# Rows brought back tile by tile at the head of the next layer, routing scratch moved, four experts with fixed weights

## What is computed

```python
y = grouped_expert_mlp(xt, expert_idx, weights, lp['e_wg'], lp['e_wu'], lp['e_wd'])
# per expert e, on the tokens sent to it: (silu(x @ wg[e]) * (x @ wu[e])) @ wd[e]
x = x + g1 * mix
x = x + g2 * hierarchical_moe(rms_norm(x, lp['norm2']) * (1 + sc2) + sh2, lp)
```

## Time and profile before

| | us |
|---|---|
| median of 3 runs (lowest, highest) | 1497.56 (1494.43, 1499.7) |
| profiled execution, its own time | 1498.07 |
| its span, first to last instruction | 1496.3 |
| PE busy | 1251.5 (84%) |
| DVE, ACT, POOL busy | 707.0, 282.6, 113.4 |
| moved by DMA | 334.61 MB, mean 224 GB/s |
| granted TensorE clock, mean | 0.92 |

### The profile page before, as it was taken

One profiled execution on the slowest core, in us unless ns is written; L12 is line 12 of the kernel. 1 busy time (PEld: TensorE's weight loads), 2 busy tenths in 40 slices (PEclk: granted clock), 3 DMA queues, 4 the chain that ended last, 5 costly groups with the idle time before them and its releaser, 6 DMA issues.

```text
span 1496.3 us, 20523 instructions
## 1 busy us (share of the span) xinstructions
PE 1251.5 (84%) x7762; PEld 860.0 (57%) x7762; DVE 707.0 (47%) x1553; ACT 282.6 (19%) x708; POOL 113.4 (8%) x171
## 2 busy tenths in 40 slices
PE   5999999889977799879739999988798569988781
PEld 2765677557863455556337556766587345655450
DVE  2256866782356133223252686677444613333224
ACT  0211233651111000000022104256221100000000
POOL 2000000000001111111100000000100011111100
PEclk7999999999977999999969999999999569999896
DMA  9221101356058999999651110023913199999975
GB/s 386 108 88 57 57 1 57 120 197 269 29 197 357 414 419 420 420 416 412 244 225 54 63 57 29 1 84 150 367 71 113 49 416 419 418 420 418 405 293 225
DMA packets 58179, 334.61 MB, mean 224 GB/s; under 512 B 11392, under 2 KB 11392, under 8 KB 23900
## 3 DMA queue, kind: packets, MB, share of 16 engines
q1 hardware_dynamic: 42336, 294.94, 48.8%
q0 software_dynamic: 15744, 38.34, 6.6%
HBM read 322.41 MB, written 27.61 MB: 234 GB/s over the span
## 4 chain that ended last, share of the span: by engine, by line
PE 50%; DMA 21%; DVE 11%; SPq 7%; issue 4%; ACT 2%; DVEq 2%; PEld 1%; POOL 0%; ACTq 0%; PEldq 0%; POOLq 0%
PE bank L1616 12%; PE bank L1560 8%; DMA ring<-in_stream 8%; PE bank L1985 7%; PE bank L1875 7%; SPq L350 6%; DMA RAB<-in_stream 6%; PE bank L2019 5%; DMA mod_rows<-RAB 2%; DMA U<-in_stream 2%; DMA RAB<-mod_rows 2%; DMA U<-moe_out 1%; PE bank L1717 1%; PE bank L1891 1%; DVE U L1168 1%
## 5 line engine op out<-in xcount | busy, mean ns | idle before, releaser
L1985 PE MATMUL bank<-U,HT 128*64 128x256 f32 (+2 forms) x1088 | 205.4, 411 | 12.5 <-DMA RAB<-in_stream 4.7
L1985 PE MATMUL bank<-ring,HT 128*64 128x256 f32 (+2 forms) x736 | 143.3, 434 | 46.0 <-DMA RAB<-in_stream 27.7
L1616 PE MATMUL bank<-HT,ring 128*128 128x512 f32 (+1 forms) x640 | 175.4, 435 | 2.0 <-issue 2.0
L1985 PEld LDWEIGHTS bank<-U,HT 128*64 128x64 f32 (+2 forms) x1088 | 131.2, 154 | 51.0 <-issue 26.4
L1875 PE MATMUL bank<-ring,HT 128*128 128x256 f32 x640 | 148.7, 394 | 13.3 <-DVE U L1219 7.7
L1560 PE MATMUL bank<-ring,HT 128*128 128x256 f32 x640 | 149.1, 385 | 3.0 <-ACT HT L603 3.0
L1875 PEld LDWEIGHTS bank<-ring,HT 128*128 128x128 f32 x640 | 125.7, 199 | 33.0 <-issue 10.0
L1616 PEld LDWEIGHTS bank<-HT,ring 128*128 128x128 f32 x640 | 97.3, 191 | 79.7 <-issue 79.7
L1985 PEld LDWEIGHTS bank<-ring,HT 128*64 128x64 f32 (+2 forms) x736 | 85.6, 154 | 91.8 <-issue 70.9
L1560 PEld LDWEIGHTS bank<-ring,HT 128*128 128x128 f32 x640 | 119.4, 192 | 18.6 <-issue 3.7
L1008 DVE SCALAR_TENSOR_TENSOR U<-U,prm 128x655 f32<-128x655 f32 x120 | 107.8, 899 | 6.3 <-issue 0.4
(11 more groups left out here) (346 smaller groups left out, 1590.4 us busy)
## 6 DMA issues: line engine op xcount, KB each, us to landing
ring<-in_stream SPq DMA_DIRECT2D x162, 1024.0 KB, 18.7
U<-in_stream SPq DMA_DIRECT2D x90, 1024.0 KB, 28.0
RAB<-in_stream SPq DMA_DIRECT2D x14, 1024.0 KB
U<-moe_out SPq DMA_DIRECT2D x20, 512.0 KB, 7.6
RAB<-mod_rows POOLq DMA_DIRECT2D x12, 512.0 KB, 11.9
moe_in<-CAT POOLq DMA_DIRECT2D x10, 512.0 KB, 3.2
X<-in_x SPq DMA_DIRECT2D x1, 2560.0 KB, 15.0
out_y<-X SPq DMA_DIRECT2D x5, 512.0 KB, 6.9
```

The source lines that it names most:

```text
L1616: ins = e.matmul(out, wt(q)[:, k, P * (n % 2):P * (n % 2) + P], HT[:, k, lo:lo + w], start=(k == 0), stop=(k == KD - 1))
L1985: ins = e.matmul(PS[2 + p][s, FF * j:FF * j + FF], xgT[:, p, k, s], wt(key)[:, k, :], start=(k == 0), stop=(k == KD - 1))
```

## The change

1. `FIXED` is 4: experts 0 to 3 have F blocks, only four B blocks are left for the largest ranked experts, and the order is `FPPFPPBPFFPQBQBBPP` (F in rounds 0, 3, 8 and 9). Twelve tiles (0 to 11) come first in SP's order.
2. SP loads tiles 5 to 10 without `lanes_rdy`, tile 11 after `h2_rdy` of all five token tiles, tile 12 after `lanes_rdy`, tile 13 after `mod_st`. The waits for `ov_go` and `wslot_ps` ahead of tile 11 are gone; `ov_go` is waited for after the last expert tile.
3. The table's scratch (`over`, `masked`, `place16`, `blockno`, `rows16`, `place`, `wblk`, `cmp`) lies in `HT`, whose content is dead by then. `lanes` is made right after the ranks instead of after the slots. The float32 `place` is written by ACT as a copy of `place16` (new semaphore `place_rdy`) in place of DVE's compare.
4. The adds of the rows for layer 0 move to the head of layer 1 and run tile by tile between squares, roots, scaling, transposes and projection tiles.

```diff
-FIXED, BIGS, MIDS, SMALLS = 2, 8, 16, 8
+FIXED, BIGS, MIDS, SMALLS = 4, 8, 16, 8
-ROUNDS = list("QFPPFBPPPBPBBQBBPP")
+ROUNDS = list("FPPFPPBPFFPQBQBBPP")
...
-                for i in range(EXT, 3 * FIXED):
+                for i in range(EXT, RING + EXT):
+                    load_expert(i)
+                e.wait_ge(S["h2_rdy"], NT * (l + 1))
+                for i in range(RING + EXT, 3 * FIXED):
                     load_expert(i)
                 e.wait_ge(S["lanes_rdy"], l + 1)
-                for i in range(3 * FIXED, RING + EXT):
-                    load_expert(i)
-
-                e.wait_ge(S["ov_go"], l + 1)
-                e.wait_ge(S["wslot_ps"], l + 1)
-                for i in range(RING + EXT, PLACES - 1):
+                for i in range(3 * FIXED, PLACES - 1):
                     load_expert(i)
                 e.wait_ge(S["mod_st"], 64 * (l + 1))
...
+                if l:            # ACT
+                    squares(0)
+                    normed_out(0)
+                    for t in range(1, 4):
+                        squares(t)
+                    qkv_out(0)
+                    normed_out(1)
+                    normed_out(2)
+                    squares(4)
+                    qkv_out(1)
+                    qkv_out(2)
+                    normed_out(3)
+                    normed_out(4)
...
+                e.wait_ge(S["slot_rdy"], l + 1)
+                A(place, place16, ACT.Copy).then_inc(S["place_rdy"], 1)
...
+                if l:            # DVE; rows_back(0, l - 1) and modc stand ahead
+                    norm1(0, 1)
+                    scaled(0)
+                    rows_back(1, l - 1)
+                    evac1(0)
+                    rows_back(2, l - 1)
+                    rows_back(3, l - 1)
+                    norm1(1, 2)
+                    scaled(1)
+                    scaled(2)
+                    evac1(1)
+                    evac1(2)
+                    rows_back(4, l - 1)
+                    norm1(3, 2)
+                    scaled(3)
+                    scaled(4)
+                    evac1(3)
+                    evac1(4)
...
+                if l:            # PE
                     normed_tile(l, 0)
+                    qkv_tile(0)
                     normed_tile(l, 1)
+                    normed_tile(l, 2)
+                    qkv_tile(1)
+                    qkv_tile(2)
+                    normed_tile(l, 3)
+                    normed_tile(l, 4)
+                    qkv_tile(3)
```

More of the change, by code:

```diff
@@ L611, in qkv_out, with squares @@
                     A(qkv[:, t, :], PS[4 + t % 2][:], ACT.Copy).then_inc(S["pj_sb"], 1)
[L613 to L616, removed]
+                def squares(t):
+                    e.wait_ge(S["x_rdy"], NT * (l - 1) + t + 1)
+                    A(nrow2, X[:, t, :], ACT.Square, accum_out=small(1400 + t, 1))
+                    e.drain()
+                    e.drain().then_inc(S["sq_rdy"], 1)
+                if l:
[11 more added lines that the diff above has]
+                    normed_out(4)
+                else:
+                    normed_out(0)
+                    normed_out(1)
+                    for t in range(NT - 2):
                         qkv_out(t)
@@ L884, in _, with norm1 @@
             for l in range(DEPTH):
+                def norm1(t0, n):
+                    e.wait_ge(S["sq_rdy"], (3 + NT) * l - NT + t0 + n)
+                    rs(n, 1.0 / D, 1400 + t0)
                 if l:
-                    e.wait_ge(S["sq_rdy"], 4 * l)
-                    rs(NT, 1.0 / D)
-                    scaled(0)
-                    scaled(1)
+                    rows_back(0, l - 1)
                 e.wait_ge(S["ld_par"], 16 * (l + 1))
@@ L904, in evac1 @@
                     ins.then_inc(S["hT_d"], 1)
-                for t in range(NT):
-                    evac1(t)
-                    if t + 2 < NT:
-                        scaled(t + 2)
+                if l:
[16 more added lines that the diff above has]
+                    evac1(4)
+                else:
+                    for t in range(NT):
+                        evac1(t)
+                        if t + 2 < NT:
+                            scaled(t + 2)
                 e.wait_ge(S["dt_act"], 3 * l + 2)
@@ L1321, in _ @@
                 e.tensor_scalar(small(1660, NE), rank, float(BIGS), 2.0, ALU.min, ALU.mult); dr()
+                e.tensor_tensor_reduce(small(1280, NE), key, iota[:, 0:NE], 1.0, 0.0, ALU.mult, ALU.add, lane)
                 e.tensor_tensor(capm, capm, step, ALU.add)
                 e.tensor_tensor(at0, at0, small(1660, NE), ALU.add); dr()
-                e.tensor_scalar(at0, at0, float(QUART), None, ALU.mult)
+                e.tensor_scalar(lane, lane, 3.0, float(experts(l)), ALU.mult, ALU.add)
+                e.tensor_scalar(at0, at0, float(QUART), None, ALU.mult); dr()
+                e.tensor_copy(lanes[:], lane).then_inc(S["lanes_rdy"], 1)
                 nov, cs, cs2 = small(1280, NE), small(1320, 16 + NE), small(1370, 16 + NE)
@@ L1368, in _ @@
                                 ALU.mult).then_inc(S["slot_rdy"], 1)
-                lane = small(1279, 1)
-                e.tensor_scalar(key, rank, rowno[:, 0, 0:1], -1.0, ALU.subtract, ALU.is_equal); dr()
-                e.tensor_tensor_reduce(capm, key, iota[:, 0:NE], 1.0, 0.0, ALU.mult, ALU.add, lane); dr()
-                e.tensor_scalar(lane, lane, 3.0, float(experts(l)), ALU.mult, ALU.add); dr()
-                e.tensor_copy(lanes[:], lane).then_inc(S["lanes_rdy"], 1)
                 for j in range(before_slots(l) - 1):
```

65 lines of the change are left out of this document (34 added, 31 removed).

## The result

| | before | after |
|---|---|---|
| median of 20 runs, us | 1498.01 | 1489.26 |
| lowest, highest | 1494.36, 1506.89 | 1482.94, 1497.39 |
| recorded ratio to before, 95% interval | | 0.9936, 0.9920 to 0.9951 |
| profiled execution, its own time (span) | 1498.07 (1496.3) | 1485.86 (1484.1) |
| PE busy, granted clock | 1251.5, 0.92 | 1248.4, 0.93 |

A forecast was written before the change was run, and what follows sets the result against it. The prediction took the weight stream to bound each expert stage. Seam 3, layer 1's stream 8 and layer 0 -1.5 sum to 9.5 us off 1498.1, giving 1488.6, as a median 1488.0; range 8 in 10: 1481 to 1496.

The forecast's parts named there:

- The bound: Each layer's expert stage is bound by the weight stream; its end depends on when the stream becomes continuous and bytes left.
- Seam, start: Between the layers: the first projection tile of layer 1 starts about 11.5 us after the first add, 10.3 us earlier.
- Seam, the wait of 4 us ahead of tile 1: Between the layers: PE waits some 4 us ahead of the second projection tile, since DVE's program sets tile 1.
- Seam, size: Between the layers: tile-by-tile work brings L1589 4.6 us earlier, less a clock charge; gain 3, between 1.5 and 4.6.
- The charge of 1.5 us for the low clock: In the seam: one projection tile after a wait runs at the lower clock, taking 1.5 us off the 4.6 gained.
- Layer 1's stream, size: Layer 1's expert stage: the weight stream becomes continuous earlier; gain 8 us, between 3 and 11.
- Layer 1's stream, cause: Tiles 6 to 11 skip `lanes`: tile 13 saves 5.7 us, `mod_st` 5.1; about 3 given back by rounds starting with F.
- it doesn't do what it says: Rival, 7%: early fixed tiles buy nothing as they block places; layer 1 gains 0, layer 0 loses 2.5; 1497.
- Layer 0's expert stage: Layer 0's stream was already full, so only the order changes: 1.5 us lost, bounds 0 and 3.
- My own mark for a wrong forecast: Expert stages: wrong if DMA share falls below 0.95 in rounds 1 to 8, the write stays at 9, or overflow rounds appear.
- The slower rival: Rival, 5%: five rolling places starve the stream in rounds 1 and 2, 19 us a layer, 38 in all: 1526.
- The sum: Whole kernel: 3 + 8 - 1.5 = 9.5 us off 1498.1 gives 1488.6, median 1488.0; the forecast keeps 55%.

## Why the forecast held, step by step

- **The bound**: right. Both expert stages follow the weight stream; what moved them was when it became continuous.
- **Seam, start** (forecast: projection tile 0 about 11.5 us after the first add): right, 11.6.
- **Seam, the wait of 4 us ahead of tile 1**: wrong. Tile 0 ended 21.7 us after the first add and not 18.3, since it ran at 0.70; and tiles 1 and 2 were scaled at 20.5 and not 22.0, since the roots of tiles 1 and 2 start as soon as DVE is done with the adds; I had them wait for a square, but the square that they need, tile 2's, is done by then. The two errors meet: projection tile 1 starts at 24.2 us (forecast 24.6), tile 2 ends at 38.2 (forecast 38.2, both without the charge for the clock). That they meet is luck.
- **Seam, size** (forecast 3, of 1.5 to 4.6): L1641 at 47.8 us after the first add; over all traces with the new seam 46.2 to 47.8, mean 47.4, for 52.2 to 53.4 with the old, mean 52.9, so 5.5 us, above the bounds. The charge of 1.5 us for the low clock was about right: it costs 1.6 by the estimate above. The term that was mis-sized is DVE's way to tiles 1 and 2, which I had end at 22.0 us and which ended at 20.5; that gain and the clock's cost went opposite ways. The rule of the Trainium skill ("TensorE: Matmul & The Clock Gate", "Why this matters for your kernels") that the clock falls back after an idle gap agrees with the rows: after a wait of 17.79 us the transposes of tile 0 took 1.94 at a clock of 0.50. The lower gain that I worked out from it, 1.6 us, did not come, because there was no second gap: tile 1 ran at 1.00.
- **Layer 1's stream, size** (forecast 8): right. 8.6 in this pair; by the means of the five traces with the change's order and waits (274.8) and the two with the old ones (282.2) 7.4. `lanes` 10.3 us earlier (forecast 10.25), the write of the modulation rows 3.6 to 4.8 from issue to release (forecast 4.5), a new hole ahead of tile 13 (9 us, forecast 10 to 15): right, the hole 1 us short. Tile 13 in about 6 us: the changed kernel's rows don't give its landing by itself. With two fixed experts it is issued at 1197.93 and in use at 1204.19, so it had landed within 6.3. In the changed kernel the broadcasts issued with it at 1200.70 still held DVE at 1209.2, 8.5 us later.
- **Layer 1's stream, cause**: half wrong. I gave the lead to the twelve tiles without `lanes`, and `lanes` itself a sentence. Five moved DVE steps alone give 8.1 of the 8.6, and the kernel with two fixed experts gives 9.1, though its write of the modulation rows took 6.7 us and tile 13 went out 10.0 us behind the gather. My sum, 10.8 gained less 3 for the F rounds, has the right shape: 13.1 and 4.5 are what the kernel with the old waits shows. But its 3 was no price of filling the hole; it was a price of the four fixed experts, and these weren't needed. The step that failed is that I costed the parts of the change only together and never asked what the early `lanes` would give by itself, though my own first paragraph had SP standing at `lanes_rdy` until tile 6.
- **The rival "it doesn't do what it says"** (fixed tiles early buy nothing, since they block places) is therefore true for the fixed tiles and false for the change.
- **Layer 0's expert stage** (forecast 1.5 lost, of 0 to 3): 285.3 to 287.7 in six traces with the order of the change, 283.0 to 285.2 in six with the old order; means 286.2 and 283.9, so 2.2 lost. In 485 to 530 us the share is 0.92 (356 GB/s) after and 1.01 (414 GB/s) before. My own mark for a wrong forecast, a share under 0.95 in rounds 1 to 8, was thus crossed in layer 0 and shortly in layer 1, and the time still held: the mark was too strict.
- **The slower rival** (five rolling places starve the stream, 1526): it didn't come. The shares of 0.92 (45 us) and 0.95 (60 us) bound what is missing at about 3 to 4 us a layer, from whatever cause, where the rival had 19. The kernel with the F rounds first shows a real starving, 6 to 9 us a layer, with no place held.
- **The sum**: by the means of the traces seam 5.5, layer 1 7.4, layer 0 -2.2, together 10.7; 9.6 by the recorded ratio (7.3 to 12.0), 8.75 by the medians. The forecast of 9.5 was made of a seam too small by 2.5, a layer 1 within 0.6, and a loss in layer 0 too small by 0.7. That the median landed 1.3 us from the forecast is partly luck.

What stays open: the changed kernel had -10.5 us on one chip and -5.7 on another, with intervals that just overlap. The clock goes with it: the mean granted clock of its executions was 0.924 (0.922 for the kernel before) on the first chip and 0.920 (0.924) on the other, which at 5.2 us for 0.01 is about 3 of the 5 us. What sets the clock from execution to execution no run here shows.

## What to carry to other kernels

Where an in-order queue of loads stands at a wait for a computed address, first ask how early that value can be made: here five moved instructions gave all that a new block table with four fixed experts gave in that layer, and the new table cost 2 us in the other. Count buffer places by what the first consumer needs before it frees any (the fourteenth place was worth 7 to 8 us in one layer and none in the other), and spread the steps that free few buffers for much PE time. A low clock on the first tile costs only what lies beyond the moment at which another engine has the second ready (here 1.6 of 2.9 us), so price it against that moment.

## What the hardware showed that I had not expected

- The same mixer work took 358 to 369 us in different executions, with DVE and ACT busy to within 0.3 us and the granted clock between 0.98 and 0.95. Two such stretches are half the program: the 6 us by which they part in a single trace are as large as most effects studied here. For whole executions of one kernel on one chip, 0.01 less granted clock went with 5.2 us more.
- A burst of 5.3 us of PE work brought the clock to 1.00, and it stood there through a wait of 2.4 us and the transposes behind it. Yet in the further wait of 2.7 us it fell, and the next 9.7 us ran at a mean of 0.72.
- The 8 KB write of POOL's took 9.9 us from issue to release with the DMA share at 1.02 meanwhile (before), 6.7 at 0.72 (two fixed experts), 4.8 at 0.38 (changed) and 3.8 at 0.47 (`lanes` early). A small write on the path to the next load was cheap here only where most of the tiles ahead of it had landed.
